# One block for the small tensors: where the buffers behind them begin

## The reference

```
first_block:   n = rmsnorm(h);  proj = n @ w_in                       # 1024 -> 2840
               o = [gated linear attention | Mamba-2 SSD] of proj     # 512 + 512
               h = h + o @ w_out
               q = rmsnorm(h) @ w_query;  top 16 of 128 keys, twice, in 8 heads
               h = h + sum over the chosen experts e of
                       gelu(x . u[e]) * gate[e] * v[e]                # 16384 experts
               h = rmsnorm(h)
second_block:  layer 0: gMLP gating;  then  f = square(relu(n @ w_up)) @ w_down   # 1024 -> 4096 -> 1024
               layer 1: banded attention over 64-token chunks; then the same MLP
```

## Time and profile before

| | |
|---|---|
| time of the kernel, median of 3 runs | 2772.78 us (2772.44 to 2777.92) |
| the profiled execution | 2774.13 us; its span from first to last instruction 2772.4 us |
| mean granted TensorE clock | 0.975 |
| PE busy | 2634.4 us, 95% of the span |
| DVE, ACT, POOL busy | 1799.7, 1034.2, 947.1 us |
| DMA | 488.35 MB, mean 176 GB/s |

### The profile page before, as it was taken

One profiled execution on the slowest core, in us unless ns is written; L12 is line 12 of the kernel. 1 busy time (PEld: TensorE's weight loads), 2 busy tenths in 40 slices (PEclk: granted clock), 3 DMA queues, 4 the chain that ended last, 5 costly groups with the idle time before them and its releaser, 6 DMA issues.

```text
span 2772.4 us, 36071 instructions
## 1 busy us (share of the span) xinstructions
PE 2634.4 (95%) x13753; PEld 2341.6 (84%) x13753; DVE 1799.7 (65%) x3033; ACT 1034.2 (37%) x1644; POOL 947.1 (34%) x528
## 2 busy tenths in 40 slices
PE   8788999899999999999999899899999999899997
PEld 6667899899999999999999877788887766788886
DVE  5643799988888878888888645660723064590542
ACT  5333334345555543333333433422223255422221
POOL 2333320014444443333333134344443412344442
PEclk9998999999999999999999899999999999999998
DMA  4222236569999989999999322232322221322331
GB/s 136 86 84 84 76 106 186 159 199 309 349 343 354 328 296 320 343 348 347 336 349 343 130 78 83 76 98 92 99 91 78 90 92 39 91 92 92 99 96 49
DMA packets 234313, 488.35 MB, mean 176 GB/s; under 512 B 85000, under 2 KB 133016, under 8 KB 233888
## 3 DMA queue, kind: packets, MB, share of 16 engines
q1 hardware_dynamic: 197280, 351.83, 39.2%
q0 software_dynamic: 36864, 134.23, 13.3%
HBM read 442.98 MB, written 42.88 MB: 175 GB/s over the span
## 4 chain that ended last, share of the span: by engine, by line
PE 82%; DVE 14%; ACT 2%; issue 1%; DMA 1%; SPq 0%; POOL 0%; DVEq 0%; ACTq 0%
PE ps L285 25%; PE ps L286 25%; PE ps L287 24%; PE ps L1525 3%; DVE wl L274 2%; DVE ti L1385 1%; DVE ti L1380 1%; PE ps L2224 1%; DVE tv L1383 1%; PE ps L2309 1%; DVE oh L1471 1%; DVE slot L1483 1%; DVE sR L1381 1%; DVE bp L1453 1%; PE ps L440 1%
## 5 line engine op out<-in xcount | busy, mean ns | idle before, releaser
L266 ACT ACTIVATE wh<-wraw 128x1024 fp32r<-128x1024 f32 x487 | 513.6, 1058 | 1338.1 <-PE ps L287 1299.5
L274 POOL TENSOR_TENSOR wl<-wraw,wh 128x1024 fp32r<-128x1024 f32 x231 | 562.9, 2442 | 957.9 <-ACT wh L266 957.9
L285 PE MATMUL ps<-Xh,wh 128*128 128x512 f32 (+1 forms) x2168 | 837.3, 386 | 42.5 <-DVE Xl L482 16.3
L286 PE MATMUL ps<-Xl,wh 128*128 128x512 f32 (+1 forms) x2168 | 797.9, 368 | 0.0
L287 PE MATMUL ps<-Xh,wl 128*128 128x512 f32 (+1 forms) x2168 | 795.4, 367 | 0.0
L285 PEld LDWEIGHTS ps<-Xh,wh 128*128 128x128 f32 x2168 | 414.3, 191 | 94.4 <-issue 27.9
L287 PEld LDWEIGHTS ps<-Xh,wl 128*128 128x128 f32 x2168 | 412.6, 190 | 47.2
L286 PEld LDWEIGHTS ps<-Xl,wh 128*128 128x128 f32 x2168 | 414.5, 191 | 44.1
L274 DVE TENSOR_TENSOR wl<-wraw,wh 128x1024 fp32r<-128x1024 f32 x256 | 312.6, 1222 | 137.6 <-ACT wh L266 129.4
L285 PE MATMUL ps<-Hh,wh 128*128 128x384 f32 x1024 | 346.8, 339 | 6.8 <-DVE Hl L1735 6.8
L287 PE MATMUL ps<-Hh,wl 128*128 128x384 f32 x1024 | 345.8, 338 | 0.0
(11 more groups left out here) (301 smaller groups left out, 3285.6 us busy)
## 6 DMA issues: line engine op xcount, KB each, us to landing
wraw<-in_uT SPq DMA_DIRECT2D x128, 512.0 KB
wraw<-in_v SPq DMA_DIRECT2D x128, 512.0 KB
wraw<-in_up SPq DMA_DIRECT2D x128, 512.0 KB
gA_scratch<-gl SPq DMA_DIRECT2D x122, 192.0 KB
gl<-gA_scratch SPq DMA_DIRECT2D x122, 192.0 KB
gG_scratch<-gbuf SPq DMA_DIRECT2D x64, 256.0 KB
lg<-gG_scratch SPq DMA_DIRECT2D x128, 128.0 KB
wraw<-in_w_q SPq DMA_DIRECT2D x24, 512.0 KB
```

The costliest lines, as they stand in the source:

```text
L266: act.activation(wh[:, n % 4, :], wraw[:, n % 4, :], ACT.Copy).then_inc(s_wh, 1)
L274: pool.tensor_tensor(wl[:, n % 4, :], wraw[:, n % 4, :], wh[:, n % 4, :].bitcast(F32), ALU.subtract).then_inc(s_wl, 1)
L285: pe.matmul(o, ah, bh, start=start, stop=False)
L286: pe.matmul(o, ah, bl, start=False, stop=False)
```

## The change

`rst4`, `warmb`, `epsc`, `leps` and `vec` become views of one tensor `small` of 160 columns, 640 bytes, which is allotted behind `iota`; and `ea1` is allotted 64 bytes in place of 4. No instruction is added, removed or reordered on any engine; the operations that used the five tensors now name `small`. What changes is the start address of everything that is allotted behind `rsb`.

```diff
     rsb = sb("rsb", [128, 3, T])
-    rst4 = sb("rst4", [128, 3, 4])
     ident = sb("ident", [128, 128])
     ones = sb("ones", [128, 128])
     iota = sb("iota", [128, 128])
-    vec = sb("vec", [128, NVEC])
-    warmb = sb("warmb", [128, 1])
-    epsc = sb("epsc", [128, 1])
-    leps = sb("leps", [128, 1])
+
+    small = sb("small", [128, 160])
+    rst4 = small[:, 0:12].rearrange("p (r c) -> p r c", c=4)
+    warmb, epsc, leps = small[:, 12:13], small[:, 13:14], small[:, 14:15]
+    vec = small[:, 16:16 + NVEC]
...
-    ea1 = sb("ea1", [8, 1], scope=mixer)
+    ea1 = sb("ea1", [8, 16], scope=mixer)[:, 0:1]
```

## The result

The changed kernel is slower, by little but clear of the noise: 2784.26 us median of 7 runs (2781.36 to 2787.38), beside 2773.99 us for the kernel before in 7 runs of the same chip (2771.88 to 2777.92). The ratio is 1.0035 with a 95% interval of 1.0024 to 1.0047, that is 6.7 to 13.0 us. Forecast were 2762.6 us, with a range of 2757 to 2774. The profiled execution took 2785.66 us, its span is 2783.9 us, 11.5 more than before.

What follows compares the result with a forecast made beforehand. PE's matmuls were taken to bound the kernel. Fh and Fl gave -10.2 us and every other term 0, so the 2772.78 us median became 2762.6 us, with an 8-in-10 range of 2757 to 2774.

Steps and rivals of the forecast that it cites:

- Fh and Fl go on the line: MLPs: 4 blocks of 384 matmuls reach the pitch of Xh, Xl, 2.55 us less each, 10.2 us in all.
- blocks of 89.6: Sign in the profile after: Fh blocks in the MLPs still at 89.6 us would mean the no-change rival.
- on and off a line of 64: MLPs: Fh, Fl start 32 bytes off a 64-byte line, touching 33 lines for 32; 6.6 ns a matmul.
- Hh and Hl go on the line: Expert passes: 3072 matmuls at 384 columns, taken as 0; 6.1 us by duration, 20.4 at Fh's price.
- at 384 columns the weight loads set the pitch: Expert passes: weight loads of 188 ns hide a slower stream, so Hh keeps 173.3 ns; argued, not shown.
- The gates: One-hot matrices: `oh` goes on the line, L1525 277 against 275 ns; at best 0.8 us, taken as 0.
- DVE: DVE and ACT buffers change alignment; taken as 0, with 8.5 us as an end if L1478 lost its quick rate.
- DMA: Stores from gbuf go off the line, gl and lg on it; no dearer per byte, taken as 0.
- No change: Rival, 16%: the start address is not what slows Fh and Fl in the MLPs; 2772.8 us.
- More: Rival, 6%: Hh and Hl in the expert passes gain too; 2742.2 us at full price, 2756.5 at 2 ns each.
- Slower: Rival, 6%: off-line gbuf stores make DMA the bound of the first expert pass; 2768 to 2807 us.
- the line: Forecast case, 72%: the 64-byte line slows Fh, Fl in the MLPs, which alone gain; 2762.6 us, 2759 to 2766.

Runs made afterwards that it cites:

- the 256-wide stream: Whole computation left out: blocks of 96 fp32r matmuls on zeros, 256 moving columns, weights 128 wide, eight start differences; 113.3 to 120.0 ns a matmul.
- the scan: Whole computation left out, PE alone: 64 blocks of 96 matmuls, moving operand's start varied; 226.7 to 234.3 ns at 512 columns, 173.3 to 176.7 at 384.
- the kernel with 256 columns: Changed kernel with `small` at 256 columns in place of 160, so Fh, Fl, Hh and Hl start at 128 modulo 512; 2765.59 us, ratio 0.9973.
- the bare stream: Matmuls without the kernel's computation, starts of weights and moving operand varied; at 512 columns 226.7 ns with equal rests modulo 256, up to 234.3 at others.

## Why the prediction was wrong

*"Fh and Fl go on the line", -10.2 us.* This is the step that failed. The blocks were rightly seen and priced: 2.5 us each is there to be had, as the runs with Fh at the weights' rest show. In the changed kernel they took 89.59 us, where the prediction had 87.1; it had named blocks of 89.6 as the sign that the address is not the cause. What was wrong is which address is a good one. The kernel before showed two start addresses only, rest 128 and rest 96 modulo 256, and I read their difference as "on and off a line of 64". That 6.6 ns are 16 columns is a coincidence: rest 0 and rest 64 are on a line and cost 5.7 and 6.7 ns.

*"Hh and Hl go on the line", 0.* Measured +7.3 of the 11.5 us of the slowdown. I had set the ends at 0 and a gain, and never asked for a loss, since the row of the kernel before showed no difference to lose. The reason given was wrong too: "at 384 columns the weight loads set the pitch". With the same loads the 256-wide stream runs at 113 to 120 ns a matmul, so loads of 188 ns overlap and set nothing at 173. PEld busy for 500 of 500 us came from overlapping spans. The pass is also longer than the prediction and the description of the kernel had it: 543.5 us from first to last start, up to 1570, and not 523 up to 1550. No number of the forecast hangs on that.

*The other steps* held. The gates: L1525 with `oh` 277 to 278 ns. DVE: L1478 at 1225 ns with tif off the line, L1631 at 1220 and 1217 ns. DMA: from 600 to 1000 us PE is busy 399.2 of 400 us, as before, and the share is 0.98 in both.

*The rivals.* "No change" was right for the Fh blocks of this change, by luck: it said that the address is not the cause, and its reasons (region, length of a chain, distance) are each refuted by the scan or by the kernel with 256 columns. "More" went the wrong way. "Slower" came true in its direction alone, and not by the stores from gbuf, whose stretch is unchanged; no rival said that an address could be made worse for a matmul. The evidence for it was at hand: Hh off the line kept its pitch and Fh off the line did not. I explained that away with the weight loads and gave the line 72%; it should have lowered every claim that rested on one pair of addresses.

*The reader's lesson in the numbers:* two points don't tell a threshold from a period. With a pattern unknown, moving 1536 matmuls from one rest to another has ends of 0 and -10.2, and moving 3072 that already run at the pitch of Xh, Xl gives no reason to hope for more and leaves room for a loss; that alone draws the middle towards no change.

## What to carry to other kernels

Where a stream of fp32r matmuls bounds a kernel, compare the pitches of stages that differ in operand address, and place the moving operands by measurement: for 128 weight columns and 512 or 384 moving ones, the same rest modulo 256 as the weights was never beaten here; the price of the other rests differed between the bare stream and the kernel in two cells, so read it from the kernel. A change of a small tensor moves every buffer behind it, so allot small ones behind the large, or pad to 256 bytes, and look at each large stage after it. An explanation of a pitch by an address wants at least a scan over starts (64 blocks, 1.3 ms) before it is priced.

## What was not expected of the hardware

- fp32r matmuls depend on the two operands' starts, with a period of 256 bytes in the scan: 226.7 to 234.3 ns at 512 columns, 173.3 to 176.7 at 384, and 113.3 to 120.0 at 256 over eight starts. The Trainium skill, "SBUF — State Buffer", section "Operand start alignment", says of its rule on starts that it is about legality, not speed, and that its runs timed nothing. In these runs the start cost nothing for bfloat16 (215.8 ns at all eight) and float32 (429.2), and up to 7.6 ns a matmul for fp32r with weights 128 wide.
- Weight loads shown as 188 ns each don't limit matmuls at a pitch of 113 ns.
- The same place of the same program spent different times at the lower clock: after the same wait of 3.8 us in the gMLP layer, the matmuls kept the pitch of 1.2 GHz for 3.5 us in one kernel and 4.8 us in the other.
